# Attention layer of a two-layer encoder: q's projection in three pieces, the key's rotation between projection pieces, the second half's keys and values without a flush ahead of them

## What is computed

```python
proj = h @ w_in                                   # 384 for q, 256 for k and v, 64 rotary
c_q, c_kv, k_rope = jnp.split(proj, [384, 640], axis=-1)
q  = (rms_norm(c_q, q_norm_g) @ w_qb).reshape(B, S, 8, 192)
kv = (rms_norm(c_kv, kv_norm_g) @ w_kvb).reshape(B, S, 8, 256)
k_nope, v = kv[..., :128], kv[..., 128:]
k = jnp.concatenate([k_nope, broadcast(k_rope)], axis=-1)
q, k = rms_norm(q, q_head_g), rms_norm(k, k_head_g)      # per head
# the last 64 of q and k are rotated by position
p = softmax(q @ k.T * 192 ** -0.5, masked by chunks of 64)
x = x + (p @ v) @ w_out
```

## Time and profile before

| | |
|---|---|
| three runs | 4060.42, 4066.88 (median), 4383.11 us |
| the profiled execution's own time | 4061.21 us |
| its span, slowest core (6) | 4059.6 us |
| spans of the eight cores | 4042.5 to 4059.6 us |
| mean granted TensorE clock | 0.988 to 0.993 |
| PE busy | 3833.1 us, 94% |
| DVE, ACT, POOL busy | 51%, 39%, 17% |

### The profile page before, as it was taken

How to read it: one execution, slowest core, us unless ns; L and a number is a source line. 1 busy time by engine, 2 the same in 40 slices (tenths; PEclk the granted TensorE clock), 3 DMA queues, 4 the chain that set the end, 5 groups by cost and what they waited for, 6 DMA issues and landing times.

```text
span 4059.6 us, 62339 instructions; the slowest of 8 cores (4042.5 to 4059.6 us)
## 1 busy us (share of the span) xinstructions
PE 3833.1 (94%) x20815; PEld 1921.6 (47%) x21200; DVE 2053.1 (51%) x3754; ACT 1593.1 (39%) x2494; POOL 676.9 (17%) x758
## 2 busy tenths in 40 slices
PE   6999999999988889999999999999999888899999
PEld 3455454444435454444454554544444454544444
DVE  3444437737354446727534445476473544467272
ACT  2432334313267564413223333443132666644030
POOL 1233221010011111110022233210000111200100
PEclk8999999999999999999999999999999999999999
DMA  6222123454332121565451221233433322324643
GB/s 157 38 57 57 27 41 49 75 89 69 65 73 64 32 68 22 98 131 110 98 130 27 51 67 24 44 65 62 89 66 66 72 53 48 74 36 75 129 72 85
DMA packets 102710, 279.43 MB, mean 69 GB/s; under 512 B 10752, under 2 KB 11904, under 8 KB 102400
## 3 DMA queue, kind: packets, MB, share of 16 engines
q0 software_dynamic: 57824, 184.84, 26.9%
q1 hardware_dynamic: 44576, 90.58, 7.3%
HBM read 426.64 MB, written 16.78 MB: 109 GB/s over the span
## 4 chain that ended last, share of the span: by engine, by line
PE 86%; issue 4%; ACT 3%; DVE 3%; DMA 2%; POOL 1%; SPq 0%; ACTq 0%; DVEq 0%; POOLq 0%; another core or an unknown queue 0%
PE psum L371 83%; PE psum L1133 2%; ACT m_P L374 1%; DMA ring<-wts 1%; DVE hT L380 1%; DMA xT<-xin 1%; POOL r_u L384 1%; ACT m_sqq L374 0%; SPq L243 0%; DVE m_ot L377 0%; DMA m_rsq<-rstd 0%; ACT rstd L374 0%; ACT n_sq L374 0%; DVE r_ab L377 0%; DVE m_rden L1141 0%
## 5 line engine op out<-in xcount | busy, mean ns | idle before, releaser
L371 PE MATMUL psum<-hT,ring 128*128 128x512 bf16 x7915 | 1784.5, 382 | 41.2 <-DMA ring<-wts 14.7
L371 PEld LDWEIGHTS psum<-hT,ring 128*128 128x128 bf16 x8064 | 790.4, 98 | 1000.2 <-issue 72.3
L377 DVE TENSOR_TENSOR xT<-xT,psum 128x512 f32<-128x512 f32 x512 | 351.0, 687 | 697.4 <-PE psum L371 678.1
L374 ACT ACTIVATE f_c<-psum,prm_s 128x512 f32<-128x512 f32 x352 | 273.3, 777 | 1034.8 <-PE psum L371 1024.2
L380 DVE SCALAR_TENSOR_TENSOR f_c<-psum,prm_s,f_c 128x511 f32<-128x511 f32 x704 | 527.1, 749 | 253.6 <-ACT f_c L374 204.0
L371 PE MATMUL psum<-f_uT,ring 128*128 128x512 bf16 x2766 | 607.4, 379 | 2.6
L243 POOL DMA_DIRECT2D ring<-wts x390 | 208.4, 540 | 2066.1 <-PE psum L371 1961.8
L374 ACT ACTIVATE m_P<-psum,m_rstdk 128x512 bf16<-128x512 f32 (+3 forms) x640 | 386.7, 625 | 151.2 <-PE psum L1133 142.5
L371 PEld LDWEIGHTS psum<-f_uT,ring 128*128 128x128 bf16 x2816 | 275.5, 98 | 332.3
L1133 PE MATMUL psum<-m_v,m_P 128*128 128x129 bf16 x2176 | 235.8, 221 | 19.5 <-DVE m_ot L377 18.2
L371 PE MATMUL psum<-r_u,ring 128*128 128x512 bf16 x976 | 242.9, 379 | 6.9 <-DVE xT L377 2.6
(11 more groups left out here) (108 smaller groups left out, 3022.6 us busy)
## 6 DMA issues: line engine op xcount, KB each, us to landing
ring<-wts POOLq DMA_DIRECT2D x250, 512.0 KB, 6.9
ring<-wts POOLq DMA_DIRECT2D x128, 352.0 KB, 4.7
m_rope<-mrope SPq DMA_DIRECT2D x40, 512.0 KB, 4.1
xT<-xin SPq DMA_DIRECT2D x32, 512.0 KB, 13.9
r_rt<-rrope SPq DMA_DIRECT2D x32, 512.0 KB, 3.9
m_rsq<-rstd SPq DMA_DIRECT2D x128, 128.0 KB, 2.3
xout<-xT SPq DMA_DIRECT2D x32, 512.0 KB, 7.6
ring<-wts POOLq DMA_DIRECT2D x4, 1024.0 KB, 9.0
```

Source lines behind the costliest of these rows:

```text
L371: return kb.op('pe', lambda e: e.matmul(out, lhsT, rhs, start=start, stop=stop), reads, writes, signal)
L374: return kb.op('act', lambda e: e.activation(out=out, in_=in_, func=func, **kw), reads, writes)
L377: return kb.op('dve', lambda e: e.tensor_tensor(out=out, in0=a, in1=b, op=op), reads, writes)
```

## The change

In the latents' loop `k_rope` of the tile before now stands between `proj(tt, [4])` and `proj(tt, [5])` instead of ahead of `q_norm`, takes banks 7 and 6 (for the last tile 6 and 0), and `N.sums` uses bank 7 instead of 6. `project` becomes three stages of three matmuls (blocks 2, 0, 1, so banks 7, 5, 6), each queueing the square of its own bank; the two stages that only squared go, one blank comes, and a chain has 13 stages instead of 12. `kv(1)` no longer follows a flush: the last `fin` runs in its iteration 1, the output chunks in iterations 4 to 7 in the banks of the keys and values, and the chain starts in iteration 1.

```diff
-            def k_rope(tt):
+            def k_rope(tt, b0, b1):
                 ts = slice(tt * 512, (tt + 1) * 512)
-                pr, prb = bank(7)
+                pr, prb = bank(b0)
...
-                pr, prb = bank(6)
+                pr, prb = bank(b1)
...
                 proj(tt, [3])
-                if tt > 0:
-                    k_rope(tt - 1)
                 q_norm(tt)
                 if tt < 2:
-                    N.sums(2 + tt, 6)
-                proj(tt, [4, 5])
+                    N.sums(2 + tt, 7)
+                proj(tt, [4])
+                if tt > 0:
+                    k_rope(tt - 1, 7, 6)
+                proj(tt, [5])
...
-            k_rope(3)
+            k_rope(3, 6, 0)
...
-                def project():
-                    load_rope(it)
+                def project(j):
+                    if j == 2:
+                        load_rope(it)
                     w, wbf = wq[G * 2 + p]
-                    for j in range(3):
-                        for c in range(3):
-                            MM(psum[:, 5 + j, :], w[:, c, j * 128:(j + 1) * 128], cq(it)[:, c, :], c == 0, c == 2,
-                               [wbf, cqb[it]], [pb[5 + j]], signal=(c == 2))
-
-                    later.append(lambda: ACT(sqq[:, 2, :], psum[:, 7, :], AF.Square, [pb[7]], [sqrb]))
-
-                def square(a):
-                    later.append(lambda: ACT(sqq[:, a, :], psum[:, 5 + a, :], AF.Square, [pb[5 + a]], [sqqb[a]]))
+                    for c in range(3):
+                        MM(psum[:, 5 + j, :], w[:, c, j * 128:(j + 1) * 128], cq(it)[:, c, :], c == 0, c == 2,
+                           [wbf, cqb[it]], [pb[5 + j]], signal=(c == 2))
+                    sb_ = sqqb[j] if j < 2 else sqrb
+                    later.append(lambda: ACT(sqq[:, j, :], psum[:, 5 + j, :], AF.Square, [pb[5 + j]], [sb_]))
...
-                stages.extend([project, lambda: square(0), lambda: square(1), sums, root, none, scale_r, turn, none,
+                stages.extend([lambda: project(2), lambda: project(0), lambda: project(1), none, sums, root, none, scale_r, turn, none,
...
-                sqkb = [ar.buf('m_sqk%d' % i, 99.5 + i, 1) for i in range(5)]
+                sqkb = [ar.buf('m_sqk%d' % i, 99.5 + i, 1) for i in range(3)]
...
-                    for _ in range(2):
+                    if i in (1, 2):
+                        while fins and (i == 2 or len(fins) > 1):
+                            fins.pop(0)[1](rotp)
+                    if i == 3:
+                        sqkb.extend(ar.buf('m_sqk%d' % j, 99.5 + j, 1) for j in (3, 4))
+                    for _ in range(2 if i > 3 else 0):
                         if todo:
-                            todo.pop(0)(roty)
-                    if i >= 1 and not begun and not todo:
+                            todo.pop(0)(rotp)
+                    if i >= 1 and not begun:
...
                     if begun:
-                        tick()
+                        if stages:
+                            stages.pop(0)()
...
-                if G == 0:
-                    while fins:
-                        fins.pop(0)[1](None)
```

## The result

The kernel after took 4122.48 us as the median of five runs (4044.45 to 4515.09), the one before 4066.88 (4060.42 to 4773.49). In three of the five runs of the kernel after, the median among them, and in two of the five of the kernel before, cores were at a lower granted clock, so 4122.48, which lies above the range of the prediction, tells of that clock and not of the change; over the other runs the ratio is 0.9955 [0.9933, 0.9976], and in a later set 0.9952 [0.9936, 0.9968]. So the change gives some 18 us, not the 31 forecast. That 4045.33 is 15 us above the forecast of 4030 has a cause in the kernel, and what follows is about that.

What follows compares the result with a forecast made beforehand. TensorE, busy 94% of the span, was taken to bound the kernel. From 4061.2 us, gains of 8.3 + 8.3 + 4.5 + 12.6 = 33.7 us, taken as 31, gave 4030 us; forecast 4012 to 4048 (0.67), range 4010 to 4062.

Steps and rivals of the forecast that it cites:

- Latents: Latents stage, both sequences: waits for bank 6 go, a smaller new one comes; 8.3 us won, bounds 18 and 2.
- The step that failed: End of the latents: the last rotation waits for DVE instead of ACT's `m_rstd` (1.75 us before), counted at nothing.
- my sentence on transfers: Transfers on SP's queue keep their order, and `load_rope` stays ahead of the first matmul; no size given.
- the 8.3 us of gain: Keys and values, kv(0) and kv(1): waits for squares, ACT and POOL and a slow stretch shrink; bounds 2 and 11.
- the way from G=0: From G=0 to kv(1): waits for `m_ot` and `m_on` filled or gone, half the slow stretch; 4.5 us, bounds 1.7 and 7.
- kv(0)'s old tail: End of kv(1): its waits for ACT, 0.77 and 0.76, come to resemble kv(0)'s one of 0.45; 0.6 us per sequence.
- 3.8 us of clock: After kv(1): nine matmuls at 0.43 us no longer slow if the waits before shrink to kv(0)'s; 1.9 us per sequence.
- Attention: The four attention passes: shorter stall ahead of the sums, less a longer wait at bank 7; 12.6 us won, bounds 28 and -5.
- -17 and +4.4: Attention passes: the stall ahead of the sums goes, 28 x 0.6 = 17 us; bank 7 between chains 1 and 2 costs 4.4.
- Rival (b): Attention: bank 7 becomes the wait at all 16 touches, 1.9 us plus a slow stretch of 1.5 each; 4077 us, chance 0.08.
- Rival (a): Latents and attention: waits only move, DVE and ACT take back nearly everything; 4048 to 4061 us, chance 0.18.
- several short ones: The clock on TensorE: waits of 1.4 us or less, several near each other, stood before each slow stretch.

Runs made afterwards that it cites:

- a later set: The kernel after, unchanged, run once more beside the kernel before on one chip: median 4045.32 us of six runs, ratio 0.9952 [0.9936, 0.9968].
- Two buffers: The kernel after with a second buffer for the table of the key's rotation, each table loaded two tiles ahead: profiled at 4038.05 us.
- the earlier rotation: The kernel after with the rotation of the tile before right behind a projection's first three blocks, banks 6 and 7: profiled at 4028.36 us.
- the latents' part with two tables: The kernel before with only the change's latents code, plus a second buffer for the key rotation's table: profiled at 4052.39 us.
- the pieces alone: The kernel before with only q's projection in three pieces and the list of 13 stages: profiled at 4049.2 us.
- kv(1)'s part alone: The kernel before with only the change's body of `kv` (last transpose and chain from iteration 1, output chunks in 4 to 7): profiled at 4051.5 us.

## Why the prediction was partly right, and where it failed

**Latents: right in the waits, the size partly by luck.** Forecast -8.3, measured -8.8. The waits for `m_t` and for bank 6 are gone, the new one for `m_ckvn` in tile 2 is 1.93 (I said 2 to 3), that for `m_ssr` 0.42 (0.6):

```profile
1151.33 1.02 PE L371 MATMUL psum<-hT,ring 128*128 128x512 bf16 x4 [1.93 <-DVE m_ckvn L380]
...
1158.06 0.59 PE L371 MATMUL psum<-m_sq,ones 128*128 128x512 bf16 x2 [0.42 <-DVE m_ssr L387]
```

But the 8.3 held 1.5 for a slow stretch that only the slowest core of before had, one of eight, so it isn't in the medians; the waits alone gave 8.8 where I had 6.8. The rest is at the end of the stage: the last rotation waits 0.61 us for DVE instead of 1.47 to 1.75 for ACT, some 1 us per sequence that I had counted at nothing.

**The step that failed** is the sentence "At the end the last rotation waits for DVE instead of ACT's `m_rstd` (1.75 before), which I count at nothing". I had followed the rotation's matmuls and its five DVE operations and not the load it ends with; my sentence on transfers looked only at q's. The room for the load went from 8.6 to 3.2 us under a landing of 4.0 to 5.4. For kv(0) I had 2.3 of the 8.3 us of gain and it lost 8.6: 10.9 of the 15.9 us between the sum of my terms, 33.7, and the 17.8 measured. Two buffers give 6.5 of it back, the earlier rotation 6.4 with another 7.0 in the latents. Of the 8.6 lost, then, 6.5 are the late table, 1.2 the rotation's new place on DVE (the latents' part with two tables against before) and 0.8 the pieces (the pieces alone).

**kv(1): the way short, the clock right but booked elsewhere.** With the way from G=0 I had 10.5 us (4.5, and 6.0 of the 8.3: 1.0 sums, 1.2 waits for ACT, 3.8 clock); measured on the way 5.5. The wait for `m_sqq` went, but a new one of 0.63 us for the chain's `rstd` came in its place, in all 16 cases (eight cores, two sequences). The flush's waits shrank as said, and the slow stretch of the earlier trace rows, in 12 of the 16 before, with them. The waits at the end did not shrink. The end of kv(1) on the slowest core:

```profile
1391.54 0.24 PE L371 MATMUL psum<-ones,m_sqk 128*128 128x1 bf16 x4 [0.58 <-ACT m_sqk L374]
1392.55 0.24 PE L371 MATMUL psum<-ones,m_sqk 128*128 128x1 bf16 x4 [0.77 <-ACT m_sqk L374]
...
1392.98 0.63 PE L371 MATMUL psum<-m_qr,m_kr 128*128 128x512 bf16 x1
1393.41 0.63 PE L371 MATMUL psum<-m_qn,m_kn 128*128 128x512 bf16 x1
```

These are 1.35 us of waits instead of 1.53 in the earlier trace rows. I took kv(0)'s old tail as the model; kv(0)'s own tail now has 0.58 and 0.77 as well. With kv(1)'s part alone the tail is as forecast, 0.45 and 0.42 us in the first sequence, and with the pieces alone kv(0)'s tail already is 0.58 and 0.77, in both sequences. So it is the pieces that bring the longer waits to both tails; with the three pieces of the first chain back in one iteration, kv(0)'s tail is 0.75 and 0.20. By my own test, kv(1) under 28 us, this step was wrong: 29.4 from 1363.3 to 1392.7.

The matmuls at half the clock here are this core's alone. Before, such a stretch began around the first score of G=1 in 15 of the 16 cases (none more than 1.2 us behind it); in the kernel after in this one, when it was run once more in six, with kv(1)'s part alone in none. So some 3.0 of the 3.8 us of clock that I had forecast came (14 stretches of 3.4 us at half the clock, on eight cores), and the stage table shows them in the second passes, which begin with the first score. They account for the 3.3 us that kv(1)'s part alone wins there.

**Attention: the sum right by luck, its terms not.** Forecast -12.6 (-17 and +4.4), measured -12.0, of which some 3.0 are kv(1)'s clock. The order with bank 7 first costs 12.0 us in this kernel, and 7.3 with the early rotation, instead of 5.4, so with the other order the pieces and kv(1)'s clock would be worth 19 to 24. (The two waits that I summed to 5.4, 0.93 and 1.92 twice, make 5.7.) And the pieces do not take from ACT's longest line, though I said that its waits would fall from 9.1 to 4 to 6 us in a pass: 7.4, 10.3, 7.5 and 10.5 us for `m_P` became 7.7, 10.8, 7.9 and 11.0. The lines for `rstd` and `m_sqq`, 1.7 us in the earlier trace rows, went. What fell besides is a line that I had not read, the value products' wait for their bank. Before, in the first pass, and with the pieces alone:

```profile
PE psum L1133 <- DVE m_ot L377: 5.0, 12, 0.7
```

```profile
PE psum L1130 <- DVE m_ot L377: 1.6, 5, 0.3
```

Over the four passes it went from 18.2 to 6.2 us with the pieces alone. How the block of nine brought about the waits of `m_ot` I have not tested.

Rival (b) had the right place: the product frees bank 7 late. It stands once in each pass, not at all four touches. On all cores that is 32 waits of 1.3 to 3.7 us. Behind the first of them on the slowest core the three `m_cqn` last 0.81 us:

```profile
1216.21 0.81 PE L371 MATMUL psum<-m_cqn,ring 128*128 128x512 bf16 x3 [1.35 <-DVE m_rsq L377]
```

In the third pass of the same core they last 1.44 us. There the second half of (b), that such a wait brings a slow stretch, is true:

```profile
3215.93 1.44 PE L371 MATMUL psum<-m_cqn,ring 128*128 128x512 bf16 x3 [2.80 <-DVE m_rsq L377]
```

Such a stretch begins at the end of 12 of the 32 waits (from 1.1 us ahead of it to 0.1 behind), all of them among the 14 that last 2.4 us or more. Rival (a), "the waits only move", at 4048 to 4061, came near the size (4045.33, inside the 4012 to 4048 of the forecast), but what was taken back was not taken where it said: DVE's part of it is the late table and bank 7, and ACT added only 1.7 us of waits for `m_P` in four passes.

**The clock.** Neither "one long wait" nor "several short ones" describes what these traces show. The level fell behind single waits of 2.4 us and more (12 of 14 above), and also at the ends of kv(1) in the kernel before, where in the second sequence no wait of the last 20 us was longer than 0.77 us. The Trainium skill, "TensorE: Matmul & The Clock Gate", section "HAM oscillation — how this bites in real kernels", tells of falls behind one long wait for data; of the falls here only the first kind is like it, and those waits are for DVE, not for a transfer. And equal waits don't give equal levels: the waits of 0.58 and 0.77 us stand at the end of kv(1) on every core and in both sequences of the kernel after, and the level fell there in 1 of 16 cases in one execution and 6 of 16 in another. What decides it is not shown.

## What to carry to other kernels

When a step is moved, list what it issues at its end, and compare for each transfer the time from issue to next use, before and after, with its landing in the page; a load that was hidden by 4 us of slack is on the path after a move of 5. Read the whole table of waits before naming the one that a change removes: a sum can be right with both of its terms wrong, and then only a kernel with one term reversed shows it. Look at all cores before you call a slow stretch a cost of the code: the slowest core had two here that most others had not. In this kernel, asking last for the bank that is freed last was worth 7 to 12 us.

## What was not expected of the hardware

With the table early, the waits of kv(0) fell by 1.2 us and its time by 3.3; the rest is the clock. The same three waits (0.42, 0.61, 1.30 us) open kv(0) in both kernels, and behind them, ahead of the wait for `m_t`, the level fell in 7 of 16 cases with one table and in 2 of 16 with two, so it does not follow from the last waits alone; what decides it stays open. One wait of 4.06 us had the lower level behind it as well. Two additions of 64x512 took POOL 2.58 us and DVE 1.40.
